# Value sums of eight sample tokens' memory attention: probabilities stationary and values moving, in 32-row strips

## The reference, cut to what matters

```
def mem_attend(qm, kv):
    scores = jnp.einsum('nthd,nmhd->nhtm', qm, kv[:, :, 0], ...) * (1.0 / math.sqrt(MEM_HEAD_DIM))
    pr = jax.nn.softmax(scores, axis=-1)
    o = jnp.einsum('nhtm,nmhd->nthd', pr, kv[:, :, 1].astype(jnp.float32))
```

## Time and profile before

| | us |
|---|---|
| median of three runs | 2577.14 |
| the profiled execution's own time | 2577.43 |
| its span (first to last instruction) | 2575.6 |
| PE matmul busy | 2427.1 |
| DVE busy | 1380.8 |
| ACT busy | 886.0 |
| POOL busy | 546.3 |

### The profile page before, as it was taken

The page is one execution under the profiler, slowest core; times in us unless marked ns, Lnnn a source line. Parts: engine busy times, 40 slices in busy tenths (PEclk is TensorE's granted clock), DMA queues, the critical chain, the costliest instruction groups (busy, mean ns, idle before and its releaser), DMA issues. The chain is left out here.

```text
span 2575.6 us, 41670 instructions
## 1 busy us (share of the span) xinstructions
PE 2427.1 (94%) x17015; PEld 2375.3 (92%) x17015; DVE 1380.8 (54%) x2274; ACT 886.0 (34%) x1820; POOL 546.3 (21%) x548
## 2 busy tenths in 40 slices
PE   4999999999999999999899799999599999999998
PEld 4899999999997899999899799989499999999998
DVE  7665665656563453444544524442855656554555
ACT  5433333344442232233321212232533333333334
POOL 2434343401010110011101100012334343420000
PEclk8999999999999999999999899999699999999999
DMA  2132222255544432122333522111022312235554
GB/s 103 50 97 63 89 67 83 80 201 186 186 151 163 157 107 70 50 65 77 100 125 110 146 91 74 42 43 40 17 80 69 97 62 90 66 119 185 186 185 171
DMA packets 164564, 266.69 MB, mean 104 GB/s; under 512 B 10101, under 2 KB 134773, under 8 KB 163992
## 3 DMA queue, kind: packets, MB, share of 16 engines
q1 hardware_dynamic: 151352, 211.99, 24.8%
q0 software_dynamic: 13024, 52.07, 6.2%
HBM read 219.18 MB, written 44.84 MB: 103 GB/s over the span
## 5 line engine op out<-in xcount | busy, mean ns | idle before, releaser
L426 PE MATMUL ps<-uh,stream_high 128*128 128x352 f32 (+1 forms) x1392 | 462.5, 332 | 19.6 <-DVEq L2405 9.1
L427 PE MATMUL ps<-uh,stream_low 128*128 128x352 f32 (+1 forms) x1392 | 451.0, 324 | 0.0
L428 PE MATMUL ps<-ul,stream_high 128*128 128x352 f32 (+1 forms) x1392 | 449.1, 323 | 0.0
L426 PE MATMUL ps<-ffn_h_h,ffn_d_h 128*128 128x352 f32 (+1 forms) x1056 | 337.0, 319 | 2.7 <-DVE ffn_d_l L714 2.7
L428 PE MATMUL ps<-ffn_h_l,ffn_d_h 128*128 128x352 f32 (+1 forms) x1056 | 336.4, 319 | 0.0
L427 PE MATMUL ps<-ffn_h_h,ffn_d_l 128*128 128x352 f32 (+1 forms) x1056 | 336.1, 318 | 0.0
L426 PEld LDWEIGHTS ps<-uh,stream_high 128*128 128x128 f32 x1392 | 267.0, 192 | 28.0 <-issue 25.6
L427 PEld LDWEIGHTS ps<-uh,stream_low 128*128 128x128 f32 x1392 | 266.8, 192 | 1.6 <-issue 1.0
L428 PEld LDWEIGHTS ps<-ul,stream_high 128*128 128x128 f32 x1392 | 266.5, 191 | 0.0
L934 DVE TENSOR_TENSOR ffn_part<-ffn_part,ps 128x258 f32<-128x258 f32 x352 | 146.6, 417 | 185.8 <-PE ps L836 124.1
L834 PE MATMUL ps<-ffn_rights,stream_high 128*128 128x258 f32 x704 | 203.5, 289 | 30.4 <-DVE ffn_rights L523 22.4
(11 more groups left out here) (322 smaller groups left out, 5529.0 us busy)
## 6 DMA issues: line engine op xcount, KB each, us to landing
ffn_raw_d<-in_w_down SPq DMA_DIRECT2D x132, 512.0 KB, 3.2
stream_raw<-in_w_in SPq DMA_DIRECT2D x25, 1024.0 KB, 5.2
ffn_hid_out<-ffn_hid SPq DMA_DIRECT2D x88, 258.0 KB, 2.7
stream_raw<-in_w_gate SPq DMA_DIRECT2D x22, 1024.0 KB, 5.1
stream_raw<-in_w_up SPq DMA_DIRECT2D x22, 1024.0 KB, 6.0
ffn_raw_h<-ffn_hid_out SPq DMA_DIRECT2D x88, 176.0 KB, 3.3
front_beside<-in_cache_mem_kv POOLq DMA_DIRECT2D x16, 512.0 KB, 4.6
ffn_raw_h<-ffn_hid_out SPq DMA_DIRECT2D x44, 164.0 KB, 3.3
```

What stands on the lines that cost most here:

```text
L426: pe.matmul(out, w_high, a_high, start=first, stop=False)
L427: pe.matmul(out, w_low, a_high, start=False, stop=False)
L428: return pe.matmul(out, w_high, a_low, start=False, stop=last)
```

## The change

The roles in the samples' value sums are swapped. The 32 probability columns of a memory tile (all samples, all heads) become the stationary operand, and a sample's 512 value columns (four heads) become the moving one. The result of sample e of a round goes to partitions 32e to 32e + 31 of bank 7; four samples fill the bank. In each strip only the rows and column blocks where sample and head agree are of use. There are two rounds of four samples. A round's bank is copied to SBUF in one copy (onto the values of the round's first sample, which are no longer needed), four 128 x 128 transposes bring it back to bank 7 with the head width on the partitions, and four small copies pick the wanted columns. Round 0 is in job unit 14, its transposes and picks in 15, round 1 in 16 and 17.

There are now eight places for values: five of their own, and for samples 5 to 7 the key buffers and `near` once all keys are done. Values 0 to 4 are loaded one by one behind keys 2 to 6, values 5 to 7 after the fourth store of the prompt's result. The larger set lies over the bias tile of group 0, so its bias loads move from the head of POOL's work to behind the second round and the last of the prompt's stores.

```diff
         def _(gp):
             keys.gpsimd(gp)
-            groups[0].load_bias(gp)
-            jobs.gpsimd(gp)
+            jobs.gpsimd(gp, groups[0])
...
-    U_TOK, U_KEYS, U_ROWS, U_COLS, U_WEIGH, U_OUT = 0, 3, 11, 13, 14, 18
+    U_TOK, U_KEYS, U_ROWS, U_COLS, U_WEIGH = 0, 3, 11, 13, 14
+    ROUNDS, STRIP = 2, 32
+    EACH = NS // ROUNDS
+    OWN_VALUES = 5
...
     def load_values(self, gp, n):
-        if n >= 2:
-            gp.wait_ge(self.weighed, n - 1)
-        gp.dma_start(self.vals[n % 2], self.c_v[:, n, :, 1, :]).then_inc(self.val_in[n % 2], 16)
+        if n >= self.OWN_VALUES:
+            gp.wait_ge(self.scored, NS)
+        gp.dma_start(self.vals[n], self.c_v[:, n, :, 1, :]).then_inc(self.val_in[n // self.EACH], 16)
...
+        r, turn = divmod(u - self.U_WEIGH, 2)
+        if 0 <= r < self.ROUNDS:
+            (self.turn_wide if turn else self.weigh)(pe, r)
+
+    def weigh(self, pe, r):
+
+        if r == 0:
             pe.wait_ge(self.cols_taken, 1)
-        pe.wait_ge(self.val_in[n % 2], 16 * (n // 2 + 1))
+        else:
+            pe.wait_ge(self.mem_taken, r)
+        pe.wait_ge(self.val_in[r], 16 * self.EACH)
+        for t in range(self.MT):
+            for e in range(self.EACH):
+                last = pe.matmul(self.m.ps[e * self.STRIP:(e + 1) * self.STRIP, 7, :], self.p_cols[:, t, :],
+                                 self.vals[r * self.EACH + e][:, t, :], start=t == 0, stop=t == self.MT - 1)
+        last.then_inc(self.weighed, 1)
+
+    def wide(self, r):
+        return self.vals[r * self.EACH][:, 0, :]
+
+    def turn_wide(self, pe, r):
+        pe.wait_ge(self.wide_taken, r + 1)
         for h in range(MH):
-            col = n * MH + h
-            for t in range(self.MT):
-                last = pe.matmul(self.m.ps[:, 7, col:col + 1], self.vals[n % 2][:, t, h * P:(h + 1) * P],
-                                 self.p_cols[:, t, col:col + 1], start=t == 0, stop=t == self.MT - 1)
-        last.then_inc(self.weighed, 1)
+            last = pe.transpose(self.m.ps[:, 7, h * P:(h + 1) * P], self.wide(r)[:, h * P:(h + 1) * P], self.m.ident[:, :])
+        last.then_inc(self.wide_turned, 1)
+
+    def pick(self, dve, r):
+
+        dve.wait_ge(self.wide_turned, r + 1)
+        for h in range(MH):
+            first = h * P + r * self.EACH * MH + h
+            step = self.STRIP + MH
+            ins = dve.tensor_copy(self.m.s_mem[:, h, r * self.EACH:(r + 1) * self.EACH],
+                                  self.m.ps[:, 7, first:first + (self.EACH - 1) * step + 1:step])
+        ins.then_inc(self.mem_taken, 1)
...
-        if u == self.U_OUT:
-            dve.wait_ge(self.weighed, NS)
-            dve.tensor_copy(m.s_mem[:, :, :], m.ps[:, 7, 0:self.ROWS].rearrange("p (n h) -> p h n", h=MH)
-                            ).then_inc(self.mem_taken, 1)
+        r, turn = divmod(u - self.U_WEIGH, 2)
+        if 0 <= r < self.ROUNDS and not turn:
+            dve.wait_ge(self.weighed, r + 1)
+            dve.tensor_copy(self.wide(r), m.ps[:, 7, :]).then_inc(self.wide_taken, 1)
+        if 0 <= r < self.ROUNDS and turn:
+            self.pick(dve, r)
...
-    def gpsimd(self, gp):
+    def gpsimd(self, gp, then):
         for n in range(2):
             self.sample.load_keys(gp, n)
-        for n in range(2):
-            self.sample.load_values(gp, n)
         self.sample.store_token(gp)
         for n in range(2):
             self.sample.load_near(gp, n)
         for n in range(2, NS):
             self.sample.load_near(gp, n)
             self.sample.load_keys(gp, n)
-        for b in range(5):
+            if n - 2 < SampleMemory.OWN_VALUES:
+                self.sample.load_values(gp, n - 2)
+        for b in range(4):
             self.prompt.store(gp, b)
-        for n in range(2, 4):
+        for n in range(SampleMemory.OWN_VALUES, NS):
             self.sample.load_values(gp, n)
-        self.prompt.store(gp, 5)
-        for n in range(4, NS):
-            self.sample.load_values(gp, n)
-        for b in range(6, TB):
+        for b in range(4, TB):
             self.prompt.store(gp, b)
+        gp.wait_ge(self.sample.weighed, SampleMemory.ROUNDS)
+        then.load_bias(gp)
         gp.wait_ge(self.prompt.stored, 16 * TB)
-        gp.wait_ge(self.sample.weighed, NS)
```

More of the change, by code:

```diff
@@ L1933, in __init__ @@
         self.weighed = st.sem("s_weighed")
+        self.wide_taken = st.sem("s_wide_taken")
+        self.wide_turned = st.sem("s_wide_turned")
         self.mem_taken = st.sem("s_mem_taken")
@@ L1975, in tensor @@
             last.then_inc(self.coled, 1)
[L1976 to L1981, removed]
-            pe.wait_ge(self.cols_taken, 1)
-        pe.wait_ge(self.val_in[n % 2], 16 * (n // 2 + 1))
-        for h in range(MH):
-            col = n * MH + h
-            for t in range(self.MT):
-                last = pe.matmul(self.m.ps[:, 7, col:col + 1], self.vals[n % 2][:, t, h * P:(h + 1) * P],
-                                 self.p_cols[:, t, col:col + 1], start=t == 0, stop=t == self.MT - 1)
-        last.then_inc(self.weighed, 1)
+        r, turn = divmod(u - self.U_WEIGH, 2)
[3 more added lines that the diff above has]
+        if r == 0:
+            pe.wait_ge(self.cols_taken, 1)
+        else:
[10 more added lines that the diff above has]
+        pe.wait_ge(self.wide_taken, r + 1)
+        for h in range(MH):
+            last = pe.transpose(self.m.ps[:, 7, h * P:(h + 1) * P], self.wide(r)[:, h * P:(h + 1) * P], self.m.ident[:, :])
[8 more added lines that the diff above has]
+        ins.then_inc(self.mem_taken, 1)
     def vector(self, dve, u):
@@ L2039, in __init__ @@
         self.sample = SampleMemory(st, m, q, cache)
-        self.sample.vals = [space.tile(SampleMemory.MT, MEM_W) for _ in range(2)]
+        self.sample.vals = [space.tile(SampleMemory.MT, MEM_W) for _ in range(SampleMemory.OWN_VALUES)]
         self.sample.keys = [space.tile(SampleMemory.MT, MEM_W) for _ in range(2)]
         self.sample.near = space.tile(2, MEM_W)
+        self.sample.vals += self.sample.keys + [self.sample.near]
         self.prompt = MemoryAttention(st, m, space, keys, q, kt, v)
@@ L2065, in over @@
         pe.wait_ge(self.prompt.res_taken, self.prompt.HALVES)
-        pe.wait_ge(self.sample.mem_taken, 1)
-    def gpsimd(self, gp):
+        pe.wait_ge(self.sample.mem_taken, SampleMemory.ROUNDS)
+    def gpsimd(self, gp, then):
         for n in range(2):
             self.sample.load_keys(gp, n)
-        for n in range(2):
-            self.sample.load_values(gp, n)
         self.sample.store_token(gp)
```

## The result

The changed kernel takes 2557.65 us in the median of four runs (2554.26 to 2559.5). The kernel before, four runs on the same chip, takes 2577.34 (2576.58 to 2578.01). The ratio is 0.9918, with a 95% interval of 0.9906 to 0.9931. The medians differ by 19.7 us, and the interval allows 17.8 to 24.2. The forecast was a gain of 14.1 us. So the direction is as forecast and the gain is larger, by more than the measurement leaves open. The time lies at the lower edge of the range and at the place of the rival "four strips at once" (2558.7).

The account below looks back on a forecast made before the run. PE, busy 94% of the span, was taken as the bound. Value sums removed 21.80, plus stall 1.42, minus added PE work 9.08, gave 14.1 us faster: 2563.0 us, range 2557.5 to 2571.

Parts of the forecast that it names:

- four strips at once: Rival for the value-sum rounds: all four strips overlap, 1.94 us a round, 18.4 us faster, 2558.7 us; chance 0.18.
- What is removed: PE, four units holding the value sums: 43.91 us would become 22.11, so 21.80 saved: 15.51 bursts, 6.29 almost all clock.
- The round: PE, 16 records of 512 columns: partial overlap, 9 steps of 0.43, 3.87 us, or 4.09 with 0.22 for changing shape.
- The clock in and behind narrow array work: PE in the rounds and the products behind them: the granted clock comes back in full, to 1.00.
- The low clock: Rival: PE falls to 1.2 GHz in the rounds, 2590 us, or about no change with partial overlap; chance 0.09.
- The change of shape: PE, at each round: switching to matmuls that use part of the array costs at most 0.22 us.
- The transposes: PE, after each round: four 128 x 128 transposes add 0.45 us.
- The stall: PE's 1.42 us idle in job unit 4 goes, since POOL has 3.62 us less ahead of the query store.
- DVE and POOL at no cost: New DVE copies and waits and moved POOL loads cost nothing; bias loads land in 3.0 us with 2 us of slack.
- The sum: Whole kernel: 21.80 + 1.42 - 9.08 = 14.1 us faster, 2563.0 us.

Follow-up runs that it names:

- run 4: The kernel before with all 64 matmuls of the samples' value sums left out, loads unchanged: 2556.33 us, ratio 0.9907.
- run 2: The changed kernel with a round's two loops exchanged, so both memory tiles of a sample come before the next sample's: 2560.36 us, ratio 0.9923.
- Run 1: The changed kernel with all four samples of a round added up in one strip, same 16 records: 2568.61 us, ratio 0.9958.
- run 6: The kernel before with only POOL's load order changed (values 0 and 1 behind `near` 0 and 1, bias behind the prompt's last store): 2575.46 us, ratio 0.9985.
- run 7: The changed kernel again, file unchanged, on another chip: 2558.97 us, ratio 0.9927 to the kernel before.
- run 8: The changed kernel with the same swap also in the sample tokens' window attention: 2553.88 us, ratio 0.9903 to the kernel before.

## Why the prediction was right in direction and short in size

By its own steps:

**What is removed: right in the sum, not in how it divides.** Forecast 21.80 us, and run 4 gives 22.12. But the 15.51 us called "the four bursts themselves", "0.11 us apiece at full clock", held bursts at 0.74 and 0.90 of the clock: 128 records at 0.11 are 14 us. At full clock the bursts are 13.96 (4 x 3.49), and the clock is 8.2 us and not 6.29. The total did not depend on this. That the clock would come back in full also held: 1.00 in all windows of the four units.

**The round: the step that failed.** The prediction had 1.72 us as the low end and 6.88 as the high, and chose 3.87 by this: "the two records of one sample must use the same strip one after the other, and if PE starts matmuls in program order only the second record of a sample overlaps the first of the next". Both ends were measured, 1.85 (four strips) and 6.98 (one). The value between them was not read from a row. It was reasoned from an assumed order of starts, and run 2 shows that the order in the program does not set the overlap: 1.88 us with it turned round. The nearest row, the 64-row matmuls at full half price, was on the side of full parallelism, and had been listed there as the argument for the rival. The rival's sum, 18.4 us and an addition of 4.78, is what came: 4.94 us added. The four units came out 4.5 us shorter than forecast (26.73 against 31.2), and 4.1 of that is this step (9.08 - 4.94). The mechanism, strips side by side, was the right one; its size was a guess, and what happened had 0.18 of chance.

**The clock in and behind narrow array work: right.** The low clock had 0.09 of chance. Run 1 is the hardest test and shows 1.00.

**The change of shape.** Taken at 0.22 us a round. From the first record on, 0.10 to 0.13 us are left over the pure streaming. Ahead of it stand 0.09 more: the first record of a round starts 0.96 us behind that of the scores in job unit 14, where a burst of before started 0.87 us behind it, and 0.53 against 0.44 us behind the transposes in job unit 16. That is 0.22 together, start-up included, so the term held. A further 0.1 of the 2.05 that a round costs in all was not followed. The Trainium skill, TensorEngine Tiling (Array Packing), Key Properties, says that a change of mode drains the engine. The trace does not show a drain as such, and by these rows it is worth at most those 0.22 us here. The Trainium skill, TensorE: Matmul & The Clock Gate, Part 3, gives a speedup of 2.38 for three column tiles. The runs agree in kind, with 2.0 for two strips (6.98 / 3.56) and 3.8 for four.

**The transposes: right.** 0.45 us forecast, 0.42 by what their two job units gained in length.

**The stall: right.** 3.62 us less ahead of `near` was the argument; `near` is issued 3.69 us sooner, and the idle time is gone both in the changed kernel and in run 6, where nothing else moved.

**DVE and POOL at no cost: right in the sum, wrong in one row.** All DVE waits are covered. The bias loads were forecast to land in 3.0 us with 2 us of slack. They took 5.8. The 3.0 was read from loads that were issued ahead of all others (864.29, the keys from 866.46); here a weight load of 1024 KB was issued within 0.1 us of them. That it was this load which held them up is likely, but no run isolates it. DVE was 1.06 us late, and PE did not wait for it. The cover named there, that PE needs the result two units later, was what held, not the slack.

**The sum.** By parts of the profiles: 22.12 + 1.42 - 4.94 = 18.6 us. The medians give 19.7 and, in run 7, 18.3; both intervals hold 18.6, so the 1.1 us between 18.6 and 19.7 need no cause. PE's wait for the new scores in the later blend stage shows how much a single execution moves elsewhere: the idle time is 8.5 us in the profile of before, 7.2 in that of after, 5.9 in run 7 and 5.1 in run 8. None of this was tied to the change.

## What to carry to other kernels

Where a vector-matrix product has many weight loads for one moving column each, make the small side stationary and stream the large one, and put independent results in separate 32-column strips: in float32 with 512 moving columns, four strips took little more than a quarter of the time of one, and their order did not matter. Count the clock with the matmuls: here bursts of 16 single-column records cost their own length and little more, bursts of 32 on average more than half as much again (22.12 us against 13.96 for four). And when a forecast sits between two measured ends, take the end that the nearest row supports, and read a transfer's duration in a stretch with the traffic that it will meet.

## What was not expected of the hardware

- Four strips run side by side without loss: 16 float32 records of 512 columns take 6.98 us in one strip, 3.56 in two, 1.85 in four. This holds although each matmul's two records share a strip.
- The same 16 records with a strip's four records one behind the other in the program take 1.88 us, and their weight loads still come as eight, four, four. Whether TensorE or something ahead of it brings this about is open.
- The clock fell from 2.4 to 1.2 GHz with no idle time on PE: during or behind seven of the eight bursts of 32 one-column records with full weight loads (0.74 in 4.66 us; 1.00 in 3.49 and then 0.69 in run 6). With bursts of 16, of 1.7 us, it stayed at 1.00, and with 7 us of 512-column records in 32 columns of the array as well. How deep the loss goes differs between executions of the same instructions (43.91 and 45.45 us for the four units).
- Four loads of 128 KB took 5.8 us each from issue to landing beside one of 1024 KB, and 3.0 where they were issued ahead of all others.
